# A sparse-attention stage on one core: projection tiles asked for one step earlier, the two compression networks one after the other, and both groups' compressed scores in one set of matmuls

## What is computed

```python
def compress(k, pe, w1, w2):                      # 15 blocks of 32 tokens, stride 16
    blk = k[cmp_idx] + pe[None, :, None, :]
    blk = blk.transpose(0, 2, 1, 3).reshape(n_cmp, G, CMP_BLOCK * dh)
    return jax.nn.silu(blk @ w1) @ w2             # 2048 -> 256 -> 64, for each of 2 groups

k_cmp = compress(kc, pe_k, ck_w1, ck_w2)
v_cmp = compress(vc, pe_v, cv_w1, cv_w2)
...                                               # 8 heads in 2 groups; scores of q against k_cmp,
                                                  # softmax, times v_cmp; plus selected and window branches
```

## Time and profile before

| | |
|---|---|
| median of 3 runs (lowest, highest) | 1047.05 us (1043.81, 1051.8) |
| profiled execution, its own time | 1047.14 us |
| its span, first to last instruction | 1045.3 us |
| TensorE busy | 1006.9 us, 96% |
| DVE, ACT busy | 641.0 us, 506.5 us |
| mean granted TensorE clock | 0.987 of full speed |

### The profile page before, as it was taken

How to read it: one execution, slowest core, us unless ns; L and a number is a source line. 1 busy time by engine, 2 the same in 40 slices (tenths; PEclk the granted TensorE clock), 3 DMA queues, 4 the chain that set the end, 5 groups by cost and what they waited for, 6 DMA issues and landing times.

```text
span 1045.3 us, 16089 instructions
## 1 busy us (share of the span) xinstructions
PE 1006.9 (96%) x6630; PEld 902.6 (86%) x6630; DVE 641.0 (61%) x873; ACT 506.5 (48%) x744; POOL 55.0 (5%) x87
## 2 busy tenths in 40 slices
PE   7998999999999999999999987999999999999996
PEld 5856788898998998888998886998998899999995
DVE  5636576567755555678866674767645366554543
ACT  6524544454544444466644482454454455344442
POOL 4000000000200000030000001010200020000000
PEclk9999999999999999999999998999999999999998
DMA  8656332255665655555554435266465446656661
GB/s 291 205 177 206 102 102 81 84 178 163 190 194 181 193 189 182 146 173 177 174 163 141 131 104 187 83 183 204 151 188 153 129 141 199 188 181 200 181 182 40
DMA packets 134568, 170.35 MB, mean 163 GB/s; under 512 B 7536, under 2 KB 98976, under 8 KB 134496
## 3 DMA queue, kind: packets, MB, share of 16 engines
q1 hardware_dynamic: 133376, 166.51, 51.7%
q10 hardware_dynamic: 576, 1.51, 0.4%
q0 software_dynamic: 544, 1.31, 0.4%
HBM read 168.26 MB, written 1.05 MB: 162 GB/s over the span
## 4 chain that ended last, share of the span: by engine, by line
PE 84%; DVE 5%; DMA 4%; ACT 3%; issue 2%; POOL 1%; SPq 0%; ACTq 0%; POOLq 0%; DVEq 0%
PE ps L338 14%; PE ps L339 13%; PE ps L340 13%; PE ps L321 7%; PE ps L364 5%; PE ps L366 5%; PE ps L365 5%; PE ps L666 5%; PE ps L665 5%; PE ps L664 5%; DMA raws<-in_w_in 3%; PE ps L411 3%; DVE parts L1345 2%; ACT parts L923 2%; DVE room L1379 1%
## 5 line engine op out<-in xcount | busy, mean ns | idle before, releaser
L1345 DVE TENSOR_TENSOR parts<-raws,parts 128x1024 fp32r<-128x1024 f32 (+1 forms) x308 | 367.9, 1211 | 279.0 <-ACT parts L923 278.1
L923 ACT ACTIVATE parts<-raws 128x1024 fp32r<-128x1024 f32 (+1 forms) x308 | 315.3, 1043 | 261.0 <-PE ps L340 127.5
L338 PE MATMUL ps<-room_r,parts 128*128 128x256 f32 x1248 | 356.0, 285 | 4.0 <-DVE parts L1345 4.0
L339 PE MATMUL ps<-room_r,parts 128*128 128x256 f32 x1248 | 351.7, 282 | 0.0
L340 PE MATMUL ps<-room_r,parts 128*128 128x256 f32 x1248 | 351.6, 282 | 0.0
L338 PEld LDWEIGHTS ps<-room_r,parts 128*128 128x128 f32 x1248 | 235.4, 189 | 10.3 <-DVE parts L1345 4.7
L339 PEld LDWEIGHTS ps<-room_r,parts 128*128 128x128 f32 x1248 | 235.4, 189 | 1.4
L340 PEld LDWEIGHTS ps<-room_r,parts 128*128 128x128 f32 x1248 | 235.4, 189 | 0.0
L364 PE MATMUL ps<-parts,room_r 128*128 128x512 f32 (+1 forms) x336 | 136.3, 406 | 3.7 <-DVE parts L1345 3.7
L366 PE MATMUL ps<-parts,room_r 128*128 128x512 f32 (+1 forms) x336 | 132.0, 393 | 0.0
L365 PE MATMUL ps<-parts,room_r 128*128 128x512 f32 (+1 forms) x336 | 131.7, 392 | 0.0
(11 more groups left out here) (184 smaller groups left out, 848.3 us busy)
## 6 DMA issues: line engine op xcount, KB each, us to landing
raws<-in_w_in SPq DMA_DIRECT2D x100, 512.0 KB, 4.2
raws<-in_w_ffn_in SPq DMA_DIRECT2D x44, 512.0 KB, 4.1
raws<-in_w_up SPq DMA_DIRECT2D x32, 512.0 KB, 4.5
raws<-in_w_down SPq DMA_DIRECT2D x32, 512.0 KB, 4.2
raws<-in_w_ffn_out SPq DMA_DIRECT2D x22, 512.0 KB, 4.2
raws<-in_w_xkv SPq DMA_DIRECT2D x16, 512.0 KB, 4.3
raws<-in_w_out SPq DMA_DIRECT2D x8, 512.0 KB, 4.1
raws<-in_w_up_ssd SPq DMA_DIRECT2D x8, 512.0 KB, 4.4
```

The costliest lines, as they stand in the source:

```text
L338: e.matmul(ps, wh, hT[0][:, k, :], start=k == 0, stop=False)
L339: e.matmul(ps, wh, hT[1][:, k, :], start=False, stop=False)
L923: e.activation(t.h, t.raw, ACT.Copy).then_inc(s["hi"], 1)
L1345: e.tensor_tensor(t.l, t.raw, t.h.bitcast(F32), ALU.subtract).then_inc(s["lo"], 1)
```

## The change

Four edits. (1) With `ahead=True` the projections rq, rk, rv and rg put the tile of their next unit on the list at the end of the unit before. The first tile of each projection is still listed at its own unit. (2) `hidden_T(0)` follows `hidden(0)` at once, `hidden_T(1)` follows `hidden(1)`; the unit that stood between the two transposes now stands after `kTc`, ahead of `vc`. ACT's copies follow the new order. (3) Both groups' compressed scores come from 8 matmuls of 128 rows and 30 columns into one bank. For that the half of `kTc` that isn't a group's own is zero: GpSimd clears `kTc` early on (a new semaphore, `no_keys`), and ACT copies the two diagonal pieces with two instructions in place of one. DVE reads the scores with the same four instructions, in another order. (4) Two units, not one, stand between `rkT` and `cmp_T(0)`; one fewer is left after the loop.

```diff
-            def tm(name, w, c0, cn, hT, ready):
+            def tm(name, w, c0, cn, hT, ready, ahead=False):
...
+                    tile_at = lambda k0: weight(w[k0 * P:(k0 + 2) * P, c0 + b0:c0 + b0 + nb], 2, nb)
+                    asked = None
                     for k0 in range(0, K, 2):
-                        w_ = weight(w[k0 * P:(k0 + 2) * P, c0 + b0:c0 + b0 + nb], 2, nb)
+                        w_ = asked or tile_at(k0)
+                        asked = None
...
                         w_.release = count if k0 + 2 == K else done(last)
+                        if ahead and k0 + 2 < K:
+                            asked = tile_at(k0 + 2)
                         yield
...
             hidden(0, a["cmp_k_w1"][0])
+            hidden_T(0)
             hidden(1, a["cmp_v_w1"][0])
-            hidden_T(0)
-            step()
             hidden_T(1)
...
                                           for c in range(2)]), "kTc", b)
+            step()
...
             out_of("kTc", ("qT", 0), ("qT", 1))
-            for g in range(2):
-                b = bank()
-                C = psum[:, b, 0:120].rearrange("p (t h c) -> p t h c", t=2, h=4)
-                r = half_of(g)
-                for t in range(2):
-                    for i in range(4):
-                        last = group(C[:, t, i, :], [(qT[r, i, t * P:t * P + P], kTc[r, 15 * g:15 * g + 15])])
-                ends(last, ("cmp", g), b)
+            b = bank()
+            C = psum[:, b, 0:240].rearrange("p (t i n) -> p t i n", t=2, i=4)
+            for t in range(2):
+                for i in range(4):
+                    last = group(C[:, t, i, :], [(qT[:, i, t * P:t * P + P], kTc)])
+            ends(last, "cmp", b)
             step(3)
...
             turn_r("rkT", rk, 0)
-            step()
+            step(2)
             cmp_T(0)
...
             for i in range(2):
                 copy_out(hid_rows[i][0:30, :], psum[0:30, where["hid", i].bank, 0:256], ("hid", i), ACT.Silu)
-            for i in range(2):
                 copy_out(hid[i], psum[:, where["hidT", i].bank, 0:60].rearrange("p (c n) -> p c n", c=2), ("hidT", i))
-            copy_out(kTc, psum[:, where["kTc"].bank, 0:30], "kTc")
+            full("kTc")
+            e.wait_ge(s["no_keys"], 1)
+            for g in range(2):
+                r, c = half_of(g), slice(15 * g, 15 * g + 15)
+                inst = e.activation(kTc[r, c], psum[r, where["kTc"].bank, c], ACT.Copy)
...
             spread(MIX, rstd[sq_of[MIX]], None)
+
+            e.memset(kTc, 0.0).then_inc(s["no_keys"], 1)
```

More of the change, by code:

```diff
@@ L44 @@
     "final_col", "gain2", "sumsq", "zsq", "rstd", "z", "zrstd", "mlp_rstd", "x_scale", "spread", "xT_hi", "xT", "y",
-    "red", "trig", "q_rot", "r_rot", "gsig", "again", "windows", "pc_sub", "pc_exp", "pc", "nmax", "weighed",
+    "red", "trig", "q_rot", "r_rot", "gsig", "again", "no_keys", "windows", "pc_sub", "pc_exp", "pc", "nmax", "weighed",
     "ret_sq", "ret_rstd", "ret", "oT_hi", "retT_hi", "gates", "mix", "mix_hi", "mixT", "up", "up_hi", "upT",
@@ L485, in tensor @@
             spread_rstd(2, MIX)
-            fill = chain(tm("rq", w_in, 1304, 512, xT, x_ready(MIX)), tm("rk", w_in, 1816, 512, xT, x_ready(MIX)),
-                         tm("rv", w_in, 2328, 512, xT, x_ready(MIX)), tm("rg", w_in, 2840, 512, xT, x_ready(MIX)),
+            fill = chain(*(tm(name, w_in, 1304 + 512 * i, 512, xT, x_ready(MIX), True)
+                           for i, name in enumerate(("rq", "rk", "rv", "rg"))),
                          fm("sig", w_in, 3352, 2048, xT, x_ready(MIX)))
@@ L1081, in scalar @@
                 copy_out(hid_rows[i][0:30, :], psum[0:30, where["hid", i].bank, 0:256], ("hid", i), ACT.Silu)
-            for i in range(2):
                 copy_out(hid[i], psum[:, where["hidT", i].bank, 0:60].rearrange("p (c n) -> p c n", c=2), ("hidT", i))
-            copy_out(kTc, psum[:, where["kTc"].bank, 0:30], "kTc")
+            full("kTc")
[3 more added lines that the diff above has]
+                inst = e.activation(kTc[r, c], psum[r, where["kTc"].bank, c], ACT.Copy)
+                if g:
+                    emptied(inst, "kTc")
+                else:
+                    step(inst)
             copy_out(vc[0:15, :, :], psum[0:15, where["vc"].bank, 0:128].rearrange("p (g d) -> p g d", g=2), "vc")
-            full(("cmp", 1))
+            full("cmp")
             e.wait_ge(s["pc_sub"], 1)
@@ L1574, in vector @@
                    col(pe_col).unsqueeze(2).unsqueeze(3).to_broadcast([P, 16, 2, 15]), ALU.add).then_inc(s["windows"], 1)
[L1575 to L1579, removed]
+            full("cmp")
+            C = bank_of("cmp")[:, 0:240].rearrange("p (t i g c) -> p t g i c", t=2, i=4, g=2)
+            for t in range(2):
+                for g in range(2):
+                    inst = stt(pc[:, t, 4 * g:4 * g + 4, :], C[:, t, g, :, :], 0.125,
                                bc(const("cmask")[:, 15 * t:15 * t + 15], 1, [P, 4, 15]), ALU.mult, ALU.add)
-                    if t:
-                        emptied(inst, ("cmp", g))
+                    if t and g:
+                        emptied(inst, "cmp")
                     else:
@@ L1585, in vector @@
             settle()
-            out_of(("cmp", 0))
-            out_of(("cmp", 1))
+            out_of("cmp")
             step(e.tensor_reduce(mxc, pc2, AX.X, ALU.max))
```

## The result

| | before | after |
|---|---|---|
| median of seven runs each (lowest, highest), us | 1047.65 (1043.81, 1052.21) | 1039.2 (1037.29, 1042.41) |
| ratio after/before, 95% interval | | 0.9911 [0.9885, 0.9938] |
| profiled execution: own time, span | 1047.14, 1045.3 | 1042.41, 1040.6 |
| TensorE busy, instructions | 1006.9, 6630 | 1005.3, 6614 |

The forecast was 1039.3. The profiled execution of after is 3.2 us above its median, so its span says 4.7 us where the medians say 8.

A forecast was written before the change was run, and what follows sets the result against it. TensorE, busy 1006.9 of 1045.3 us, bounds the kernel, with 6.2 us of waits in the edited stage. 6.1 us up to `cmp` plus 1.6 of late waits make 7.7 off: median 1039.3, range 1034 to 1047.

The forecast's parts named there:

- The stage: From the first `hidden()` to the end of `cmp`: it ends at 92.5 in place of 98.58, -6.1 us.
- The walk: TensorE followed through the edited stage, 2.95 us per unit, 3.64 for two whole tiles, to place each wait.
- Compressed scores: At `cmp`: 16 instructions in 1.7 us in place of 32 in 3.32, -1.6 us (bounds -1.2 and -1.6).
- The clock: Behind `vc`, 85 to 100 us: with only short idle pieces the granted clock stays at 1.00, saving 1.3 us.
- The late waits: At S3 (1.26) and the transpose of head 1's probabilities (0.85): one more unit ahead of `cmp_T(0)` gains 1.6 us.
- The fit of 3.7 against 3.9 us: Ahead of head 1's transpose: the chain from `cmp_T` takes 3.7 us, covered by 3.9 us of TensorE work.
- The slower rival: Compression tiles asked for too late: 1057 with landings of 10 us, deciding from about 8 us; chance 0.05.
- shortfalls: Time by which compression tiles' loads land after their use: 19 us at 10 us landings, 8.5 at about 8.
- Landings above 6.5 us: Loads near 60 us taking over 6.5 us to land, named as one thing that would prove the forecast wrong.
- the cover of 9.6 us: At v0: its load is asked for 9.6 us ahead of its use.
- faster by over 1%: Whole kernel gaining more than 1%, 10.5 us: half of the second rival and a quarter of the forecast, chance 0.18.

The follow-up runs named there:

- edit (4) alone: The kernel before with only two units in place of one ahead of `cmp_T(0)`, one fewer after the loop: 1050.04 us, ratio 0.9994.

## Why the prediction was right

- **The stage.** Predicted for the end of `cmp`: 92.5 - 55.69 = 36.8 us behind the first `hidden()`. Measured 36.3 (57.51 to 93.81, where the next unit begins), 38.1 and 35.9 in the three traces of the changed kernel, 42.8 before. The walk held because its pieces did: no wait ahead of rk's units, none at the first transpose, 0.42, 0.47 and 0.16 at the second (0.55 predicted), 0.24, 0.48 and 0 at `vc` (0.2), k12 late by 0.2 (3.86 for 3.64), 1.55 and 0.17 (0.65).
- **Compressed scores.** -1.6 predicted; measured 1.86 us in place of 3.32, and from its start to the next unit's 1.71 in place of 3.25, so -1.5. By the rule of the Trainium skill that different tiles load and run in parallel (TensorEngine Tiling (Array Packing), Key Properties) it could have been 0; the trace of the kernel before, with 32 instructions one after the other in 3.32 us, has no overlap to lose.
- **The clock.** That it would hold between 85 and 100 was right in every trace with all four edits, and in none of the four traces with one edit alone: behind the hidden rows it fell in all seven traces in which `kTc` and `vc` together waited 2.1 to 3.6 us, and in none of the seven in which they waited up to 1.1.
- **The late waits.** This term was mis-sized: 1.6 predicted, 0.96 in the profile after (2.11 less 0.73 and 0.42), 1.14 with edit (4) alone. The fit of 3.7 against 3.9 us ahead of the transpose was too optimistic, because ACT rounds two tiles in a row behind its copies (2.02 us at 110.59), and the silu that moved ahead of a copy was not priced.
- **What wasn't seen.** The wait ahead of q stood at 0.62 in the kernel before; I took it as given. It depends on how early TensorE gets there: 1.8 to 3.3 us in the five traces that arrive by 48.6 us, four of them with edit (1) and one without, and 0.4 to 0.6 in the five later ones, one with edit (1). The profiled execution of before was a late one and that of after an early one, so 1.1 of its 2.04 us take back what the quicker start had given; the rest comes with the rotation, which begins 0.95 us later (48.99 against 48.04). A part of that may belong to edit (1): from its load's issue to ACT's rounding rk's first tile takes 5.0 us on average in the five traces with it and 4.5 in the five without, and the rotation starts 0.65 us later. Nothing of edit (1) comes ahead of that tile in any engine's list, and whether this is chance is open.
- **The slower rival.** It asked for landings of 8 us at all the compression tiles. (At 8 us its shortfalls add up to 8.8 and not 8.5, which changes nothing.) Landings above 6.5 us were named as a sign against the forecast. They came in all three traces of the changed kernel, at v0: 7.0, 8.0 and 6.9. With the cover of 9.6 us worked out for it they cost nothing. What did cost something was k12, with 4.7 us of cover: 6.3 us to land in one trace, below the sign's mark, and 1.55 us of waiting. The sign was put at the wrong place; it should have been put at the tile with the least cover.
- **Two small slips.** Half of 0.12 and a quarter of 0.55 are 0.20 for faster by over 1%, not 0.18. GpSimd clears `kTc` at 18 us, 70 us ahead of its copy and not 40. Neither bears on the time.
- The median agrees with 1039.3 to 0.1 us partly by luck: 0.6 too much in the late waits, differences between executions of 1 to 2 us, and the pace at the start of the program, which the prediction didn't look at.

## What to carry to other kernels

Where one list gives both the order of the loads and the order of the splitting work, write out the list before and after, and walk TensorE with measured durations: each wait that goes and each that comes can be named ahead. Look at what a copy on ACT has queued ahead of it by plan; a copy that TensorE wants at once shouldn't stand behind roundings that wait for loads. And read the DVE's idle time ahead of a critical operation too: one tile's rest put behind it brought 1.5 and 1.9 us in the medians of two sets of runs, in the changed kernel; in the kernel before it showed nothing. When a wait differs between two traces, look first at when each engine arrived there, back to the start of the program, before the change is blamed.

## What was unexpected

Waits at the same place differ in what follows: 2.04 and 1.95 us ahead of the transposes of q were followed by a granted clock of 0.66 from 50 to 55 us (2.4 and 1.2 GHz mixed), 2.62 + 0.63 in a third trace of the same kernel by 1.00. And the same three loads of 512 KB (k12, rk4 and v0, issued within 1 us) took 4.8, 6.2 and 7.0 us to land in one execution and 6.3, 7.2 and 8.0 in another, with nothing changed in the kernel. Last, kernels that are the same up to there start their first projection at either pace, and the 1 to 3 us that this is worth on the way to the transposes of q are partly waited away there.
